# A fused two-layer block on one core: the second expert's columns in their own bank, half of them ahead of the first expert's turn

## Chip, cores and metric

The kernel runs on one core of a Trainium2 chip. The metric is the device time of one execution in microseconds (us), as the median of several. A core has TensorE (PE in the profile, PEld for its weight loads), VectorE (DVE), ScalarE (ACT), GpSimd (POOL) and SyncE (SP), which issues the DMAs. They meet at semaphores.

## What is computed

Two transformer-like layers in fp32 for 256 tokens of width 1024. The first has latent attention, retention, cross attention and a hierarchical mixture of experts, the second a gated recurrence, a short convolution, a SwiGLU block and a per-layer embedding gate. The change is in the mixture of experts:

```python
g_sel = jnp.argmax(g_logits + b_group, axis=-1)              # 1 of 4 groups for a token
e_logits = jnp.take_along_axis(e_all, g_sel[:, None, None], axis=1)[:, 0]
_, top_idx = lax.top_k(e_logits + e_bias, TOP_K)             # 2 of its 8 experts
gate = one_hot(g_sel) * local_w * g_w                        # zero for the other experts
a = jnp.einsum('sd,edf->sef', hr, w_gate)
u = jnp.einsum('sd,edf->sef', hr, w_up)
act = jax.nn.silu(a) * u * gate
return jnp.einsum('sef,efd->sd', act, w_down)                # width 256 inside an expert
```

## The kernel before

**Precision.** Products are done in fp32r. Each operand is split in a high part, rounded to fp32r, and a low part, the rest; a product is three matmuls (`three`, lines 2363 to 2367: high by high, high by low, low by high). The weights come from memory in units of 128 x 2048 floats. ScalarE makes a unit's high part `w_hi` in two halves (`split_hi`, line 440), VectorE its low part `w_lo` in two halves (`split_lo`, line 454), each waiting for the half before it on the other engine. `w_hi` and `w_lo` are rings of three units: the split of unit u waits until TensorE is done with unit u - 3 (`unit_done`). The landing places (`stage`, `first`, `second`, `third`) are six in this stage: SyncE issues the load of a unit once the low part of the unit six before it is ready (`slot_free`, line 395).

**Experts.** Tokens are sorted by group into 128 slots for each of four groups. All eight experts of a group run over the group's 128 slots, so 32 steps in all. An expert has three units: two for the gate and up columns (halves of the 1024 inputs; the 512 result columns of gate and up lie in one PSUM bank, `bank[6]`) and one down unit. Of the first expert (`j` = 0) these are units base, base + 1 and base + 4, of the second base + 2, base + 3 and base + 7: the down unit stands behind the next expert's columns.

A step of TensorE (`step(g, j)`, line 2977) does expert j's columns (24 matmuls), then the down unit of expert j - 1 (12 matmuls into banks 4 and 5), then `turn_hidden`: it transposes expert j's hidden values into bank 7. The columns of the next expert, into bank 6 again, wait for `expert_hidden`, that is until bank 6 is read. ScalarE in the meantime does `tanh` of the gate columns out of bank 6, splits, and copies the turned values to `aT_hi`; VectorE does the two element-wise steps to `silu_g` and `hidden` (lines 2095 and 2097), splits, and makes `aT_lo`.

At g's end `bring_back` multiplies the group's result `y` by the matrix that takes slots to tokens, and adds to banks 0 to 3. These are opened ahead by `open_sums`, a product of a matrix of zeros with `start=True` for each bank: banks 1 to 3 before the first turn, bank 0 after the first down unit, because bank 0 still holds the gates of groups 1 to 3 until ScalarE has copied them (`moe_slot_gates`).

**Order.** `expert_steps` (line 666) writes the order on each engine: steps (0,0) and (0,1) straight; then a loop over g of the steps 2 to 9 (steps 8 and 9 are the next group's first two); then the last group's rest straight. TensorE runs it as a loop of three passes, ScalarE and VectorE have all of it straight. In step (0,0) TensorE also transposes `slot_of` and makes the gates (`turn_gates`), the later ones after ScalarE has kept the gathered tokens of later groups (`later_kept`), which is the last read of banks 0 to 3 from the gathering. In step 0 ScalarE's order is: tanh, split of base + 3, `aT_hi`, gates of groups 1 to 3, two copies to `token_of`; then step 1 with the splits of base + 4 and base + 5, and tanh. VectorE's: `silu_g`, `hidden`, split of base + 3, `aT_lo`; then base + 4, base + 5, `silu_g`, `hidden`.

## Time and profile before

| | us |
|---|---|
| median of three runs | 935.25 |
| lowest and highest | 935.12, 936.57 |
| profiled execution: time | 936.84 |
| profiled execution: its span in the profile | 934.9 |
| TensorE busy | 925.4 |
| VectorE busy | 742.9 |
| ScalarE busy | 625.4 |
| experts' stage on TensorE | about 240 to 521 |

The rows below are from the profiled execution; its time is 1.9 us longer than its span, for what lies around it. A row of a timeline gives start, duration, engine, line, operation, output and inputs, shapes and a count; in brackets stands how long the engine was idle before it, and whom it waited for. Matmuls are pipelined: the duration of one (0.39 us for 512 columns) holds its latency, and the distance between starts, some 0.23, is what the engine takes.

### The profile page before, as it was taken

To read this page: it belongs to the slowest core of one execution; us is meant where nothing else is said; L and a number is where in the kernel's file an instruction comes from. 1 tells how busy PE (TensorE), PEld (TensorE's weight loads), DVE (VectorE), ACT (ScalarE), POOL (GpSimd) and SP (SyncE) were. 2 spreads that over 40 slices of the span, in tenths; PEclk is the share of its full clock that TensorE was granted. 3 is DMA by queue.
4 is the path that set the end of the run, shared out by engine and by line. 5 is a ranking of instruction groups with operands and counts; after the bars stand their busy time and mean duration, and the time that the engine had idled before them with its cause. 6 is when DMAs were issued, how large, how long until landed. Compare 5 with 4: busy or idle time off the path is not lost.

```text
span 934.9 us, 13599 instructions
## 1 busy us (share of the span) xinstructions
PE 925.4 (99%) x5025; PEld 801.7 (86%) x5025; DVE 742.9 (79%) x1111; ACT 625.4 (67%) x953; POOL 20.5 (2%) x41
## 2 busy tenths in 40 slices
PE   9999999999999999999999999999999999999997
PEld 7888888888888888888888899999998888888886
DVE  6667687678999999999999889898897655555576
ACT  6685686676878778788777765747575544434456
POOL 2500000000000000000000000000000000000000
PEclk9999999999999999999999999999999999999999
DMA  9755427523799999999999364737457566555531
GB/s 341 243 183 187 148 91 253 174 70 136 250 371 372 354 363 374 356 366 375 353 365 325 99 198 157 251 114 243 154 186 244 184 201 198 180 180 180 187 129 45
DMA packets 102766, 214.50 MB, mean 229 GB/s; under 512 B 5672, under 2 KB 60480, under 8 KB 97088
## 3 DMA queue, kind: packets, MB, share of 16 engines
q1 hardware_dynamic: 101072, 211.70, 65.3%
q0 software_dynamic: 1344, 2.01, 0.8%
q8 instruction: 26, 0.43, 0.2%
q10 hardware_dynamic: 304, 0.20, 0.1%
q14 instruction: 20, 0.16, 0.0%
HBM read 212.84 MB, written 1.05 MB: 229 GB/s over the span
## 4 chain that ended last, share of the span: by engine, by line
PE 93%; DMA 2%; DVE 2%; ACT 1%; SPq 0%; issue 0%; DVEq 0%; ACTq 0%
PE bank L2367 20%; PE bank L2365 20%; PE bank L2366 20%; PE bank L3196 6%; PE bank L3198 6%; PE bank L3197 6%; PE bank L2382 4%; DMA stage<-in_cross_w_kv_dram 2%; PE bank L2378 2%; PE bank L2372 2%; PE bank L2373 1%; PE bank L2718 1%; PE bank L3223 0%; PE bank L3224 0%; PE bank L3222 0%; DVE w_lo L467 0%
## 5 line engine op out<-in xcount | busy, mean ns | idle before, releaser
L2365 PE MATMUL bank<-w_hi,xT_hi 128*128 128x512 f32 (+2 forms) x626 | 246.9, 394 | 0.0
L2367 PE MATMUL bank<-w_hi,xT_lo 128*128 128x512 f32 (+2 forms) x626 | 242.3, 387 | 0.0
L2366 PE MATMUL bank<-w_lo,xT_hi 128*128 128x512 f32 (+2 forms) x626 | 242.1, 387 | 0.0
L2367 PEld LDWEIGHTS bank<-w_hi,xT_lo 128*128 128x128 f32 x626 | 117.6, 188 | 24.0
L2365 PEld LDWEIGHTS bank<-w_hi,xT_hi 128*128 128x128 f32 x626 | 118.1, 189 | 21.9 <-DVE w_lo L467 0.2
L2366 PEld LDWEIGHTS bank<-w_lo,xT_hi 128*128 128x128 f32 x626 | 117.8, 188 | 22.0
L465 DVE TENSOR_TENSOR w_lo<-stage,w_hi 128x1024 fp32r<-128x1024 f32 (+3 forms) x94 | 107.4, 1142 | 30.2 <-ACT w_hi L451 28.8
L3196 PE MATMUL bank<-hT_hi,w_hi 128*128 128x256 f32 x440 | 123.7, 281 | 0.0
L3198 PE MATMUL bank<-hT_hi,w_lo 128*128 128x256 f32 x440 | 123.6, 281 | 0.0
L3197 PE MATMUL bank<-hT_lo,w_hi 128*128 128x256 f32 x440 | 123.5, 281 | 0.0
L451 ACT ACTIVATE w_hi<-stage 128x1024 fp32r<-128x1024 f32 (+3 forms) x96 | 95.5, 995 | 31.0 <-PE bank L2367 13.3
L467 DVE TENSOR_TENSOR w_lo<-stage,w_hi 128x1024 fp32r<-128x1024 f32 (+3 forms) x94 | 107.1, 1139 | 0.0
L452 ACT ACTIVATE w_hi<-stage 128x1024 fp32r<-128x1024 f32 (+3 forms) x96 | 94.8, 987 | 0.0
L446 ACT ACTIVATE w_hi<-stage 128x1024 fp32r<-128x1024 f32 x55 | 58.2, 1058 | 42.6 <-PE bank L2367 42.3
L459 DVE TENSOR_TENSOR w_lo<-stage,w_hi 128x1024 fp32r<-128x1024 f32 x54 | 65.8, 1219 | 25.1 <-ACT w_hi L446 25.0
L3196 PEld LDWEIGHTS bank<-hT_hi,w_hi 128*128 128x128 f32 x440 | 83.0, 189 | 0.0
L3197 PEld LDWEIGHTS bank<-hT_lo,w_hi 128*128 128x128 f32 x440 | 83.0, 189 | 0.0
L3198 PEld LDWEIGHTS bank<-hT_hi,w_lo 128*128 128x128 f32 x440 | 83.0, 189 | 0.0
L2367 PE MATMUL bank<-w_hi,aT_lo 128*128 128x512 f32 x204 | 79.7, 391 | 0.0
L2365 PE MATMUL bank<-w_hi,aT_hi 128*128 128x512 f32 x204 | 79.6, 390 | 0.0
L2366 PE MATMUL bank<-w_lo,aT_hi 128*128 128x512 f32 x204 | 79.4, 389 | 0.0
L461 DVE TENSOR_TENSOR w_lo<-stage,w_hi 128x1024 fp32r<-128x1024 f32 x54 | 65.8, 1219 | 0.0
(488 smaller groups left out, 1520.8 us busy)
## 6 DMA issues: line engine op xcount, KB each, us to landing
stage<-in_w_in_dram SPq DMA_DIRECT2D x36, 1024.0 KB, 5.2
stage<-in_w_gate_up_dram SPq DMA_DIRECT2D x44, 512.0 KB, 4.7
stage<-in_expert_w_gate_dram SPq DMA_DIRECT2D x33, 512.0 KB, 5.5
stage<-in_expert_w_up_dram SPq DMA_DIRECT2D x33, 512.0 KB, 6.4
second<-in_expert_w_down_dram SPq DMA_DIRECT2D x16, 1024.0 KB, 6.8
stage<-in_expert_w_down_dram SPq DMA_DIRECT2D x15, 1024.0 KB, 7.1
stage<-in_w_down_dram SPq DMA_DIRECT2D x11, 1024.0 KB, 4.8
stage<-in_w_out_dram SPq DMA_DIRECT2D x8, 1024.0 KB, 6.0
```

The source lines that it names most:

```text
L451: nc.scalar.activation(w_hi[:, s, 0:half], src[:, 0:half], ACT.Copy).then_inc(st.half_ready, 1)
L452: nc.scalar.activation(w_hi[:, s, half:cols], src[:, half:cols], ACT.Copy).then_inc(st.hi_ready, 1)
L459: nc.vector.tensor_tensor(beside(w_lo, s, 0), of_both(st, u0, 0), beside(w_hi, s, 0).bitcast(F32), ALU.subtract)
L461: nc.vector.tensor_tensor(beside(w_lo, s, 1), of_both(st, u0, 1), beside(w_hi, s, 1).bitcast(F32), ALU.subtract).then_inc(st.lo_ready, 1)
L465: nc.vector.tensor_tensor(w_lo[:, s, 0:half], src[:, 0:half], w_hi[:, s, 0:half].bitcast(F32), ALU.subtract)
L467: nc.vector.tensor_tensor(w_lo[:, s, half:cols], src[:, half:cols], w_hi[:, s, half:cols].bitcast(F32), ALU.subtract).then_inc(st.lo_ready, 1)
L2365: mm(o, k_hi, v_hi, start=start, stop=False)
L2366: mm(o, k_hi, v_lo, start=False, stop=False)
L2367: return mm(o, k_lo, v_hi, start=False, stop=stop)
L3196: mm(o, w_hi[:, s, at:at + P], hT_hi[:, k, :], start=k == 0, stop=False)
L3197: mm(o, w_hi[:, s, at:at + P], hT_lo[:, k, :], start=False, stop=False)
L3198: ins = mm(o, w_lo[:, s, at:at + P], hT_hi[:, k, :], start=False, stop=k == KD - 1)
```

## The change

The second expert of the first group (`second_expert`: main stream, g the integer 0, j = 1) gets bank 3 for its columns; ScalarE and VectorE read it there. TensorE does the first half of them at the end of step (0,0), before the turn of the first expert's hidden values, and the second half at the head of step (0,1), with no wait for `expert_hidden`. On ScalarE and VectorE the split of the first down unit (base + 4) moves from the head of step (0,1) into step (0,0), behind the split of base + 3 and ahead of `aT_hi` and `aT_lo`. `open_sums` and its four products of zeros are gone: the first `bring_back` starts each bank itself. For that g must be a plain integer in the first pass, so TensorE's first pass over the loop is written out (`peeled=1`), and the loop runs over the two others. The wait for `moe_slot_gates` moves ahead of the first `bring_back`.

```diff
--- before.py
+++ after.py
@@ -663,7 +663,7 @@
 
 
 
-    def expert_steps(eng, groups, step, tail, straight=False):
+    def expert_steps(eng, groups, step, tail, straight=False, peeled=0):
 
         step(0, 0)
         step(0, 1)
@@ -672,7 +672,10 @@
                 for j in range(2, PER_GROUP + 2):
                     step(g, j)
         elif groups > 1:
-            with eng.Fori(0, groups - 1) as g:
+            for g in range(peeled):
+                for j in range(2, PER_GROUP + 2):
+                    step(g, j)
+            with eng.Fori(peeled, groups - 1) as g:
                 for j in range(2, PER_GROUP + 2):
                     step(g, j)
         for j in range(2, PER_GROUP - 1):
@@ -708,6 +711,14 @@
         return k // 2 * 2 + 2
 
     EMBED_ORDER = ((1, 0), (1, 1), (0, 0), (0, 1))
+
+    def second_expert(st, g, j):
+
+        return st is main and isinstance(g, int) and (g, j) == (0, 1)
+
+    def expert_columns(st, g, j):
+
+        return bank[3 if second_expert(st, g, j) else 6]
 
     def gate_bank(g):
 
@@ -1417,12 +1428,14 @@
                 act.wait_ge(st.unit_done, g * PER_TURN + (up_unit(base, j) + 1))
                 if j == PER_GROUP:
                     act.wait_ge(sem(name + "_slot_gates"), 2)
-                nc.scalar.activation(silu_t[:, 0], bank[6][:, 0:FF], ACT.Tanh,
+                nc.scalar.activation(silu_t[:, 0], expert_columns(st, g, j)[:, 0:FF], ACT.Tanh,
                                      scale=slot_gates[:, bass.ds(scale_column(g, j), 1)]).then_inc(sem("expert_tanh"), 1)
                 if j == LAST and next_up:
                     next_high(g, 1)
                 if next_up:
                     split_hi(act, SLOT, up_unit(base, j + 1), PER_TURN, g, st)
+                    if second_expert(st, g, j + 1):
+                        split_hi(act, SLOT, up_unit(base, 1) + 1, PER_TURN, g, st)
                 if last_down_unit is not None and splits[0]:
                     splits[0]()
                 act.wait_ge(sem("expert_turned"), eighths(g, e0 + j + 1))
@@ -1436,7 +1449,7 @@
                     nc.scalar.activation(y_hi[:, c], by_block(bank[4 + c]), ACT.Copy).then_inc(sem("expert_y_hi"), 1)
 
             def step(g, j):
-                if j:
+                if j and not second_expert(st, g, j):
                     split_hi(act, SLOT, up_unit(base, j) + 1, PER_TURN, g, st)
                 if j or st is not main:
                     split_hi(act, SLOT, gate_unit(base, j + 1), PER_TURN, g, st)
@@ -2092,14 +2105,17 @@
                 if last_down_unit is not None:
                     chunk_lo(dve, last_down_unit, 0, st)
                 dve.wait_ge(sem("expert_tanh"), eighths(g, e0 + j + 1))
-                stt(silu_g[:, 0], silu_t[:, 0], 1.0, bank[6][:, 0:FF], ALU.add, ALU.mult).then_inc(sem("expert_silu"), 1)
+                columns = expert_columns(st, g, j)
+                stt(silu_g[:, 0], silu_t[:, 0], 1.0, columns[:, 0:FF], ALU.add, ALU.mult).then_inc(sem("expert_silu"), 1)
                 dve.wait_ge(sem("expert_silu"), eighths(g, e0 + j + 1))
-                stt(hidden[:, 0], bank[6][:, FF:2 * FF], slot_gates[:, bass.ds(gate_column(g, j), 1)], silu_g[:, 0],
+                stt(hidden[:, 0], columns[:, FF:2 * FF], slot_gates[:, bass.ds(gate_column(g, j), 1)], silu_g[:, 0],
                     ALU.mult, ALU.mult).then_inc(sem("expert_hidden"), 1)
                 if j == LAST and next_up:
                     next_low(g, 1)
                 if next_up:
                     split_lo(dve, SLOT, up_unit(base, j + 1), PER_TURN, g, st)
+                    if second_expert(st, g, j + 1):
+                        split_lo(dve, SLOT, up_unit(base, 1) + 1, PER_TURN, g, st)
                 if last_down_unit is not None:
                     chunk_lo(dve, last_down_unit, 1, st).then_inc(st.lo_ready, 1)
                 dve.wait_ge(sem("expert_aT_hi"), eighths(g, e0 + j + 1))
@@ -2120,7 +2136,7 @@
                     tt(dst, dst, bank[n][:, :], ALU.add).then_inc(sem(signal), 1)
 
             def step(g, j):
-                if j:
+                if j and not second_expert(st, g, j):
                     split_lo(dve, SLOT, up_unit(base, j) + 1, PER_TURN, g, st)
                 if j or st is not main:
                     split_lo(dve, SLOT, gate_unit(base, j + 1), PER_TURN, g, st)
@@ -2890,12 +2906,12 @@
                         ins = mm(bank[6][:, :], xg_lo[:, kk], w_hi[:, s, at:at + 512], start=False, stop=kk == KD - 1)
                     ins.then_inc(st.unit_done, 1)
 
-            def columns_of(half, u0, g):
+            def columns_of(half, u0, g, j):
                 pe.wait_ge(st.lo_ready, g * PER_TURN + (u0 + 1))
-                s = u0 % RING
+                s, o = u0 % RING, expert_columns(st, g, j)[:, :]
                 for k in range(4):
                     kk = 4 * half + k
-                    ins = three(bank[6][:, :], xg_hi[:, kk], xg_lo[:, kk], w_hi[:, s, 512 * k:512 * k + 512],
+                    ins = three(o, xg_hi[:, kk], xg_lo[:, kk], w_hi[:, s, 512 * k:512 * k + 512],
                                 w_lo[:, s, 512 * k:512 * k + 512], start=kk == 0, stop=kk == KD - 1)
                 ins.then_inc(st.unit_done, 1)
 
@@ -2949,40 +2965,35 @@
                 for c in range(2):
                     pe.wait_ge(sem("expert_y_hi"), g * 2 + (c + 1))
                     for t in range(T):
-                        mm(bank[2 * c + t][:, :], tokens[t], y_hi[:, c], start=False, stop=False)
+                        mm(bank[2 * c + t][:, :], tokens[t], y_hi[:, c], start=isinstance(g, int) and g == 0, stop=False)
                     pe.wait_ge(sem("expert_y_lo"), g * 2 + (c + 1))
                     for t in range(T):
                         ins = mm(bank[2 * c + t][:, :], tokens[t], y_lo[:, c], start=False, stop=last)
                         if last:
                             ins.then_inc(sem(name + "_returned"), 1)
 
-            def open_sums(banks):
-
-                for n in banks:
-                    mm(bank[n][:, :], zeros[:, 0:P], slot_of[:, 0], start=True, stop=False)
-
             def gate_up(g, j):
-                if j:
+                if j and not second_expert(st, g, j):
                     pe.wait_ge(sem("expert_hidden"), eighths(g, j))
                 if j == PER_GROUP:
                     pe.wait_ge(sem(name + "_moved"), g * 2 + 1)
                 if j == 0:
                     first_columns((gate_unit(base, j), up_unit(base, j)), g)
                     return
-                columns_of(0, gate_unit(base, j), g)
+                if not second_expert(st, g, j):
+                    columns_of(0, gate_unit(base, j), g, j)
                 if j == PER_GROUP:
                     pe.wait_ge(sem(name + "_moved"), g * 2 + 2)
-                columns_of(1, up_unit(base, j), g)
+                columns_of(1, up_unit(base, j), g, j)
 
             def step(g, j):
                 gate_up(g, j)
                 if j == PER_GROUP + 1:
+                    if isinstance(g, int) and g == 0:
+                        pe.wait_ge(sem(name + "_slot_gates"), 2)
                     bring_back(g)
                 if j:
                     down(g, j - 1, up_unit(base, j) + 1)
-                    if j == 1:
-                        pe.wait_ge(sem(name + "_slot_gates"), 2)
-                        open_sums((0,))
                 else:
                     pe.wait_ge(sem("places_known"), 2 * T + 1)
                     for n in range(groups):
@@ -2995,7 +3006,7 @@
                     turn_gates(range(1))
                     pe.wait_ge(sem("later_kept"), KD)
                     turn_gates(range(1, groups))
-                    open_sums((1, 2, 3))
+                    columns_of(0, gate_unit(base, 1), g, 1)
                 turn_hidden(g, j)
 
             def tail(g):
@@ -3005,7 +3016,7 @@
                 down_by_chunks(g, last_down(base, groups))
                 bring_back(g, last=True)
 
-            expert_steps(pe, groups, step, tail)
+            expert_steps(pe, groups, step, tail, peeled=1)
 
         flags = []
         experts("moe", main, U_MOE, GROUPS)
```

## Rows read from the trace of the kernel before

**Rows 1.** Page of the profile, busy time of the engines

```profile
PE 925.4 (99%) x5025; PEld 801.7 (86%) x5025; DVE 742.9 (79%) x1111; ACT 625.4 (67%) x953; POOL 20.5 (2%) x41
```

**Rows 2.** Busy by stretch: us, PE, PEld, DVE, ACT, POOL, PEclk, DMA share, GB/s

```profile
257.70:266.10 8.40, 8.40 (x41) 6.98 (x40) 8.37 (x10) 6.67 (x8) 0.00 (x0) 1.00 1.01 368
```

**Rows 3.** Waits, 230 to 300 us: engine, waited for: us in total, times, longest

```profile
PEld bank L2382 <- DVE hidden L2097: 0.6, 2, 0.4
```

**Rows 4.** Timeline of PE: start us, us, engine, line, op, tiles, count, idle before

```profile
247.83 0.95 PE L2962 MATMUL bank<-slot_of,zeros 128*128 128x512 f32 x3
...
248.78 0.51 PE L2382 MATMUL bank<-const,hidden 128*128 128x128 f32 x2
...
249.04 0.48 PE L2365 MATMUL bank<-w_hi,xT_hi 128*128 128x512 f32 x1
...
254.60 0.39 PE L2365 MATMUL bank<-w_hi,aT_hi 128*128 128x512 f32 x1
...
257.32 0.40 PE L2962 MATMUL bank<-slot_of,zeros 128*128 128x512 f32 x1
...
257.55 0.39 PE L2382 MATMUL bank<-const,hidden 128*128 128x128 f32 x2
...
257.70 0.48 PE L2365 MATMUL bank<-w_hi,xT_hi 128*128 128x512 f32 x1
```

**Rows 5.** Timeline of ACT (ScalarE), 247 to 251 us

```profile
247.33 1.05 ACT L446 ACTIVATE w_hi<-first 128x1024 fp32r<-128x1024 f32 x1
...
248.28 1.05 ACT L448 ACTIVATE w_hi<-first 128x1024 fp32r<-128x1024 f32 x1
...
249.33 0.39 ACT L1430 ACTIVATE aT_hi<-bank 128x256 fp32r<-128x256 f32 x1
...
249.70 1.10 ACT L1450 ACTIVATE token_of<-bank 128x512 fp32r<-128x512 f32 x2
...
250.65 1.08 ACT L451 ACTIVATE w_hi<-second 128x1024 fp32r<-128x1024 f32 x1
```

**Rows 6.** Timeline of DVE (VectorE), 246 to 257 us

```profile
246.66 1.22 DVE L461 TENSOR_TENSOR w_lo<-stage,w_hi 128x1024 fp32r<-128x1024 f32 x1
...
249.78 1.22 DVE L461 TENSOR_TENSOR w_lo<-first,w_hi 128x1024 fp32r<-128x1024 f32 x1
...
250.91 0.42 DVE L2107 TENSOR_TENSOR aT_lo<-bank,aT_hi 128x256 fp32r<-128x256 f32 x1
...
251.77 1.23 DVE L465 TENSOR_TENSOR w_lo<-second,w_hi 128x1024 fp32r<-128x1024 f32 x1 [0.44 <-ACT w_hi L451]
...
256.32 0.41 DVE L2095 SCALAR_TENSOR_TENSOR silu_g<-silu_t,bank 128x256 f32<-128x256 f32 x1
...
256.77 0.48 DVE L2097 SCALAR_TENSOR_TENSOR hidden<-bank,slot_gates,silu_g 128x256 f32<-128x256 f32 x1
```

**Rows 7.** Timeline of DVE and PEld at the fourth expert's turn

```profile
273.79 0.48 DVE L2097 SCALAR_TENSOR_TENSOR hidden<-bank,slot_gates,silu_g 128x256 f32<-128x256 f32 x1
...
274.33 0.31 PEld L2382 LDWEIGHTS bank<-const,hidden 128*128 128x128 f32 x2 [0.20 <-DVE hidden L2097]
```

**Rows 8.** Timeline of DVE, its next wait after 251.77

```profile
295.62 1.22 DVE L459 TENSOR_TENSOR w_lo<-stage,w_hi 128x1024 fp32r<-128x1024 f32 x1 [0.18 <-ACT w_hi L446]
```

**Rows 9.** Loads into `second`, 245 to 520 us, from issue to landing

```profile
DMA to landing us min/median/max: 4.8/6.7/8.3
```

**Rows 10.** Timeline of PE around a loop edge and the loop's exit

```profile
316.77 0.48 PE L2365 MATMUL bank<-w_hi,xT_hi 128*128 128x512 f32 x1
...
327.07 0.48 PE L2365 MATMUL bank<-w_hi,xT_hi 128*128 128x512 f32 x1
...
455.48 0.48 PE L2365 MATMUL bank<-w_hi,xT_hi 128*128 128x512 f32 x1
...
465.79 0.48 PE L2365 MATMUL bank<-w_hi,xT_hi 128*128 128x512 f32 x1
```

**Rows 11.** DMA queues, 240 to 325 us: packets, MB, share of 16 engines

```profile
q8 instruction: 4, 0.07, 0.3%
```

## Prediction

> **What bounds the kernel now.** I read the page first: TensorE is busy for 925.4 of 934.9 us [rows 1], so only what lies on its own path can move the end. Then the busy times by stretch: inside the experts' stage TensorE is never idle, its clock is the full 2.4 GHz (granted 1.00), VectorE is busy for 8.37 of 8.40 us and the DMA engines are full (share 1.01) [rows 2]. So there are three candidates for a bound, and the question is which of them the change meets next. Then the waits of TensorE, of which the second expert's start holds one of 0.4 us, on the first expert's hidden values [rows 3]. Last the three engines' timelines between 246 and 258 us, where nearly all of the change happens.
>
> I call the experts' units U+0, U+1 (first expert's columns), U+2, U+3 (second's), U+4 (first down unit), U+5, U+6 (third's columns), U+7 (second down unit).
>
> TensorE now ends the gate products, opens three banks with products of zeros at 247.83, waits for `hidden` and turns it at 248.78, starts the second expert's columns at 249.04, the first down unit at 254.60, opens bank 0 at 257.32, turns the second hidden at 257.55 and starts the third expert at 257.70 [rows 4]. A dozen products without a restart takes 257.32 - 254.60 = 2.72 us; the dozen after a turn takes 254.60 - 249.04 - 2.72 = 2.84. Where the turn is late, its first weight load starts 0.06 us after `hidden` ends (274.33 against 273.79 + 0.48) [rows 7] and the columns 0.26 after the turn (249.04 - 248.78), 0.32 in all. A turn that isn't late takes 257.70 - 257.55 = 0.15.
>
> **The products of zeros and the idle time.** Between 247.83 and 248.78 lie three products of zeros and a wait, 0.95 us, and bank 0's product costs 257.55 - 257.32 = 0.23 [rows 4]. The most that can go is 1.18 us. The `start` flag that replaces them is on products that are issued anyway, and the wait for the slot gates, moved to `bring_back`, is met some 60 us before: ScalarE has those copies behind it when it starts `token_of` at 249.70 [rows 5]. Both at nothing.
>
> **Half the second expert's columns ahead of the turn.** They need U+2's low parts: the last VectorE half of it starts at 246.66 and takes 1.22, so 247.88 [rows 6]; with 0.06 for the signal TensorE starts at 247.94 instead of 247.83. Then 2.84 to 250.78. Bank 3 instead of 6 is what makes this free of the readers of bank 6; bank 3's own last readers are the copies to `later`, for which the gate products wait already. The turn follows at 250.78 without a wait. The other half needs U+3's low parts: 249.78 + 1.22 = 251.00 [rows 6], so it starts at 251.06, not at 250.93: 0.13 lost. It ends at 253.90.
>
> **The down unit's split ahead of the turned values.** On ScalarE the halves of U+3 start at 247.33 and 248.28, 0.95 apart [rows 5]. U+4 follows at 249.23 and 250.18, not at 250.65 [rows 5]; its ring place was free since the first columns ended. Queued behind it is now the copy `aT_hi`: the turn at 250.78 plus 0.43 gives 251.21, and ScalarE is free at 251.13, so nothing waits. That copy and the gates take 0.37 (249.33 to 249.70), the two `token_of` copies 0.95: ScalarE starts U+5 at 252.53 and, at some 1.07 a half, the first is there at 253.60. VectorE does U+4 from 250.91 (its place after U+3 [rows 6]), two halves of 1.14 to 253.19; behind them is `aT_lo`, 0.34, to 253.53, so the first down unit has its operand at 253.61 (the write takes 0.42). TensorE arrives there at 253.90: the margin is 0.29. VectorE then waits to 253.64 for U+5's high half: 0.11 idle where it now has 0.44 by its row and 0.52 by its starts [rows 6]. U+5 ends at 253.64 + 2.28 = 255.92, where `silu_g` starts; now it starts at 256.32. **VectorE is 0.40 us ahead, and no more**: its work is the same, only this gap closed. The tanh stands behind U+5's halves on ScalarE, at about 254.4 (the columns are done by then), and U+5's low halves hide it.
>
> **TensorE after it.** The down unit ends at 253.90 + 2.72 = 256.62; `hidden` of the second expert is ready 0.40 earlier, 256.77 + 0.48 - 0.40 = 256.85, so the third expert starts at 256.85 + 0.32 = 257.17 instead of 257.70: 0.53 gained, with the wait for zeros gone and one for VectorE in its place. Without that wait it would be 256.77, 0.93 gained.
>
> **What is late next.** From 251.77 to beyond 274 VectorE works without a gap (the next wait that its timeline shows is at 295.62 [rows 8]), and at 274.33, ahead of the fifth expert, `hidden` is already what comes last [rows 7]. There TensorE can gain only what VectorE gained: 0.40. By 295.62 VectorE has begun to wait for the others, and all moves together. The sum: -1.18 (zeros and wait) - 0.11 (the turn is not late: 0.15, not 0.26) + 0.11 (U+2) + 0.13 (U+3) + 0.12 (a restart, 2.84 for 2.72) + 0.40 (`hidden`, second expert) + 0.13 (`hidden`, fourth) = -0.40 us. For the profiled execution, 936.84 - 0.40 = 936.44; that execution lies 1.6 us above the median of the runs, 935.25, from which I count: 934.85.
>
> **Weights.** U+4's place in the stage comes free at 253.27 instead of 254.13, so its next load is issued 0.86 earlier, the others up to 0.4. A load into `second` lands within 8.3 us at most [rows 9], and a place is filled again every six units, two steps of some 8.4 us. Even with the engines full this doesn't bind, and the view of the waits has no split in this stage behind a landing. Nothing.
>
> **The peeled code.** Eight steps of TensorE stand straight ahead of the loop. Step to step, the pass over the loop's edge takes 327.07 - 316.77 = 10.30 us, and leaving the loop for straight code 465.79 - 455.48 = 10.31 [rows 10]: the edge costs nothing, and one edge less gives nothing. The copy must be fetched: four instruction blocks over 85 us took 0.3% of 16 engines, about 1.0 us each [rows 11], and the timeline shows no gap of TensorE at them. The copy adds three or four such blocks, in the same full DMA load. I take nothing; the bounds are below nothing by 0.1 (register work of the waits) and above by 4 us.
> The Trainium skill, "Runtime: NRT & Kernel Launch", section "Instruction fetch mechanics", says that a taken branch out of the window of fetched pages stalls for a fetch, and that kernels prefer unrolling for this. By it one edge less would be worth a fetch; the two passes of [rows 10] do not agree with it for this loop. The same section says that sequential prefetch mostly hides a block's crossing, which speaks against the rival of slow fetches; the straight parts here agree.
>
> **Rivals.**
> - A, all waits vanish: TensorE gains 0.95 to 1.18, 934.1 to 934.3. It needs VectorE to be shorter too; its unbroken row of work speaks against it.
> - B, nothing is gained: the copies on ScalarE (`aT_hi`, `token_of`) come later than I place them, U+5's split with them, and VectorE's gap is only moved. If U+5's first half is 0.40 us later, the whole gain is gone: 935.25. The margins of 0.1 to 0.3 us above speak for it, that each step has its row speaks against it.
> - C, slower: the blocks of the peeled copy arrive late under full DMA queues. It decides once a block lands later than TensorE's lead; three or four blocks of 1.0 us less 0.40 give +2.6 to +3.6: 938 to 939. The straight first pass of now, with its four blocks and no gap, speaks against it.
> - D, a back edge costs a fetch after all and one less gives about 1.0 more: 935.25 - 0.40 - 1.0 = 933.85. The rule of the "Instruction fetch mechanics" section above would have it so.
>
> **How the numbers follow.** Forecast 0.70, A 0.07, B 0.14, C 0.04, D 0.03, the rest 0.02. The three runs of before span 1.45 us, more than the gain, so the range takes in A and B with some 0.3 to 0.8 us of scatter: 934.0 to 936.0. A measurement of this kernel can tell about 0.2%, 1.9 us, from no change; the forecast, A, B and D lie within it (D at its edge with scatter). So faster 0.02, same 0.93, slower 0.05.
>
> **What the profile after would show.** Second expert's first product at about 247.9 into its own bank; no products of zeros; the turn at 250.8; a wait of 0.3 us or so before the turn at 256.9 for `hidden`; third expert at 257.2; fifth expert at 274.2; from there every row 0.4 us earlier, with about 8.4 us a step. VectorE without the 0.44 gap. Four instruction blocks more and no gap of TensorE beside them. It is wrong if a gap stands beside a block, if the third expert starts later than 257.7, or if the lead at 330 us isn't the lead at 520.

## The result: 0.22% slower, and a profile that hides why

| | before | changed |
|---|---|---|
| median of nine runs, us | 935.27 | 938.06 |
| lowest and highest | 934.81, 936.57 | 936.37, 939.35 |
| profiled execution, time and span | 936.84, 934.9 | 936.37, 934.5 |

The ratio is 1.0022, 95% interval 1.0013 to 1.0030: 2.8 us slower, where 0.4 us faster was forecast, and outside the range. Yet the profiled execution of the changed kernel is the quickest of its nine runs, 0.47 us below that of before. So the profile has to be read piece by piece.

**The piece that the change is about came out as summed.** TensorE's timeline of the changed kernel, 246 to 257 us (start, duration, engine, line, operation, count, idle before):

```profile
246.78 0.82 PE L2888 MATMUL bank<-token_gates,slot_of 128*128 128x16 f32 x6
247.52 0.50 PE L2381 MATMUL bank<-w_hi,xT_hi 128*128 128x512 f32 x1
...
250.39 0.39 PE L2398 MATMUL bank<-const,hidden 128*128 128x128 f32 x2
250.63 0.50 PE L2381 MATMUL bank<-w_hi,xT_hi 128*128 128x512 f32 x1
...
253.50 0.39 PE L2381 MATMUL bank<-w_hi,aT_hi 128*128 128x512 f32 x1
...
256.53 0.50 PE L2398 MATMUL bank<-const,hidden 128*128 128x128 f32 x2
256.79 0.48 PE L2381 MATMUL bank<-w_hi,xT_hi 128*128 128x512 f32 x1
```

They answer to [rows 4]. This execution was already 0.38 us ahead when it came to the experts (its first gate product starts at 245.743, that of before at 246.127), which isn't the change's. With 0.38 added, the second expert's columns start at 247.90 (said: 247.94), their second half at 251.01 (251.06), the down unit at 253.88 (253.90), the third expert at 257.17 (257.17). The products of zeros are gone. VectorE's and ScalarE's rows of the same stretch, which answer to [rows 5, 6]:

```profile
252.77 0.42 DVE L2123 TENSOR_TENSOR aT_lo<-bank,aT_hi 128x256 fp32r<-128x256 f32 x1
253.26 1.23 DVE L459 TENSOR_TENSOR w_lo<-third,w_hi 128x1024 fp32r<-128x1024 f32 x1
...
255.54 0.41 DVE L2109 SCALAR_TENSOR_TENSOR silu_g<-silu_t,bank 128x256 f32<-128x256 f32 x1
255.99 0.48 DVE L2111 SCALAR_TENSOR_TENSOR hidden<-bank,slot_gates,silu_g 128x256 f32<-128x256 f32 x1
```

```profile
250.81 0.39 ACT L1443 ACTIVATE aT_hi<-bank 128x256 fp32r<-128x256 f32 x1
...
252.14 1.09 ACT L446 ACTIVATE w_hi<-third 128x1024 fp32r<-128x1024 f32 x1
```

VectorE's idle time ahead of the split, marked 0.44 in [rows 6], is no longer marked; `hidden` is the last to come for the turn, as forecast. And the row that answers to [rows 7]: VectorE hands over `hidden` at 273.01 + 0.48, and TensorE has waited 0.33 for it.

```profile
273.54 0.32 PEld L2398 LDWEIGHTS bank<-const,hidden 128*128 128x128 f32 x2 [0.33 <-DVE hidden L2111]
```

To compare executions without their different starts I take the time from the first gate product to the last product of a `token_now` behind the experts: 521.19 - 246.13 = 275.06 us before, 520.46 - 245.74 = 274.72 changed. **The stage is 0.34 us shorter**; the sum said 0.40.

**The loss lies behind the stage.** TensorE, 520 to 526 us, first before, then changed:

```profile
520.85 0.73 PE L2955 MATMUL bank<-xT_lo,token_now 128*128 128x512 f32 x2
522.04 2.29 PE L2382 MATMUL bank<-const,x 128*128 128x128 f32 x16 [0.46 <-DVE x L2120]
524.09 0.36 PE L3208 MATMUL bank<-hT_hi,w_hi 128*128 128x256 f32 x1
```

```profile
520.12 0.74 PE L2971 MATMUL bank<-xT_lo,token_now 128*128 128x512 f32 x2
521.32 1.74 PE L2398 MATMUL bank<-const,x 128*128 128x128 f32 x11 [0.46 <-DVE x L2136]
525.04 0.71 PE L2398 MATMUL bank<-const,x 128*128 128x128 f32 x5 [1.98 <-issue]
525.50 0.36 PE L3219 MATMUL bank<-hT_hi,w_hi 128*128 128x256 f32 x1
```

Sixteen transposes follow one another; only the ninth's weight load waits, 0.34 us for VectorE's `x`. Before, they run through; now TensorE stops after the eleventh, for 1.98 us, and the reason given is "issue": nothing that the profile knows was waited for. From start to start the gap is 525.04 - 522.78 = 2.26 us, where 0.11 is usual. Nothing in the diff touches these lines. The lead of 0.72 us (522.04 against 521.32) turns into a lag of 1.41 (524.09 against 525.50).

**Why the profiled time hides it.** Busy times by stretch of the heads' stage, first before, then changed:

```profile
531.00:696.00 165.00, 165.00 (x1390) 164.88 (x1389) 144.38 (x211) 106.61 (x146) 0.00 (x0) 1.00 0.59 190
```

```profile
531.00:696.00 165.00, 164.91 (x1402) 164.58 (x1401) 145.06 (x216) 107.75 (x147) 0.00 (x0) 1.00 0.59 191
```

With TensorE busy throughout in both and the same clock, the execution of before did 1390 products in 165 us, that of the changed kernel 1402: 118.6 ns a product against 117.3, by the mean distance of their starts with the few pauses left out. From its first product to its last the stage takes 171.34 us in the one (524.09 to 695.43) and 169.50 in the other (525.50 to 695.00), 1.8 us less, and that has nothing to do with the change: of the fourteen executions profiled in this study three have the short spacing (the changed kernel here, e2 and e7, 117.3 to 117.5) and eleven the long one (118.4 to 118.7), and the changed kernel, profiled again as e8, had the long one. So the two profiles' difference of -0.47 is -0.72 (lead) + 2.13 (stop, from lead to lag) - 1.8 (spacing), and -0.1 that I leave unassigned. What the change is worth is told by the medians of nine runs, not by the two profiled executions.

### The profile page after: what moved, and what is told of

It reads as the page before. It is cut to its first block, busy times and chain, and to the rows that moved or that the text cites. A ratio compares the mean times of both kernels' runs of the same rounds, so it can differ in the third digit from the quotient of the medians.

```text
span 934.5 us, 13561 instructions
## 1 busy us (share of the span) xinstructions
PE 922.5 (99%) x5021; PEld 798.9 (85%) x5021; DVE 742.8 (79%) x1111; ACT 625.5 (67%) x953; POOL 20.6 (2%) x41
## 4 chain that ended last, share of the span: by engine, by line
PE 93%; DVE 3%; ACT 2%; issue 1%; DMA 0%; DVEq 0%; ACTq 0%
PE bank L2383 20%; PE bank L2381 20%; PE bank L2382 20%; PE bank L3207 5%; PE bank L3208 5%; PE bank L3209 5%; PE bank L2398 4%; PE bank L2394 3%; PE bank L2388 2%; PE bank L2389 2%; PE bank L2734 1%; DVE w_lo L467 1%; DMA silu_g<-in_mem_norm_g_dram 0%; DVE w_lo L465 0%; PE bank L2461 0%
```

## What stops TensorE there

Behind the experts stands code for tokens that don't fit their group's slots: two branches (lines 3102 and 3105 of the changed kernel, 3091 and 3094 before) jump over it when there are none, as here. Between the last `token_now` product and the transposes TensorE therefore takes two jumps. In the built file of TensorE's program an instruction is 64 bytes, and the trace's queue 8 ("instruction") brings packets of 16,384 bytes, so blocks of 256 instructions. I counted from the head of that file where the jump lands: at instruction 4177 before, with 175 instructions left in that block; at 4810 in the changed kernel, 633 further on because of the peeled steps, with 54 left. TensorE stopped after eleven transposes. Each is two instructions (weights, product), so 22 of the 54 are theirs; a label and a wait ahead of the first, a wait ahead of the ninth, and the weight load of the twelfth (which is done ahead of the stop) make 26.

So TensorE stops 28 instructions ahead of the place where the count puts the block's end. The same 28 remain in e1 (17 of 45 done), e3 (27 of 55) and e6 (42 of 70) below. I read this as the end of a block all the same, at the same place in every kernel, and as a count that begins 28 instructions late: in the running program every place lies 28 further on in its block than in the file. What the 28 are isn't on record. "Left", in the names of the runs and in the expectations, is the count of the file.

The theories ahead of the first experiments were:
- Theory 1: the block behind the one that the jump lands in is asked for too late, and comes some 3.7 us after TensorE goes on there. Position alone decides.
- Theory 2: the moved work does it, by other transfers at that time.
- Theory 3: peeling as such does it, by the number of blocks to be brought.

## Experiments on the cause

**e1: the peeled steps alone.** The kernel before with one pass of TensorE's loop written straight, all else as it was:

```diff
-            with eng.Fori(0, groups - 1) as g:
+            for g in range(peeled):
+                for j in range(2, PER_GROUP + 2):
+                    step(g, j)
+            with eng.Fori(peeled, groups - 1) as g:
...
-            expert_steps(pe, groups, step, tail)
+            expert_steps(pe, groups, step, tail, peeled=1)
```

> The kernel before with TensorE's first pass over the experts' loop written out, nothing else; it does 642 instructions more for TensorE, and the jump over the unused overflow code lands 45 instructions ahead of the end of its block of 256. Theory 1 (the next block is asked for only when the one landed in is entered, and comes some 3.7 us later): TensorE stops for 2.0 to 2.7 us amid the transposes behind the experts, as in the changed kernel, and the time is 1.9 us above before, or 3.6 where the clock falls after the gap: 937.2 to 939. Theory 2 (the gap belongs to the moved columns, their waits or the first products that now start the banks): no gap, 935.3. Theory 3 (the peeled steps themselves run slower, as rival C of the prediction had it): steps of more than 8.43 us between 257 and 327, no gap behind the experts.

Measured: 940.61 us against 936.91 of the kernel before, measured beside it, ratio 1.0047 (1.0032 to 1.0062), more than theory 1 had said. TensorE stops for 3.14 us from start to start (said: 2.0 to 2.7), earlier among the transposes, with 45 instructions left:

```profile
521.53 0.98 PE L2385 MATMUL bank<-const,x 128*128 128x128 f32 x7 [0.46 <-DVE x L2123]
525.38 1.18 PE L2385 MATMUL bank<-const,x 128*128 128x128 f32 x9 [2.86 <-issue]
```

The seven transposes are 14 of the 45; with the label, the wait and the eighth weight load 17 are done, and 28 are over: the stop is at the same place of a block again. Its stage takes 275.06 us, exactly that of before: the peeled steps give nothing in themselves, and one back edge less is worth nothing.

**e2: the moved work alone.** The changed kernel with TensorE's loop whole, so that the banks are opened by products of zeros as before:

```diff
-            expert_steps(pe, groups, step, tail, peeled=1)
+            expert_steps(pe, groups, step, tail)
...
+                    open_sums((1, 2))
```

> The change without the peel: the second expert's columns in bank 3, half of them ahead of the first turn, the down unit's split ahead of the turned values, but the loop of three passes kept and the four products of zeros too (banks 1 and 2 ahead of those columns, bank 0 ahead of the second turn, bank 3 behind it). The place of the code behind the experts is as before, to one instruction. Theory 1: no gap behind the experts; the third expert starts about 0.25 us earlier and the end moves by -0.2 to -0.3: 935.0. Theory 2: a gap of about 2 us behind the experts, 937 or more. Theory 3: as theory 1.

Measured: 935.78 against 936.91, ratio 0.9997 (0.9989 to 1.0006), no gap behind the experts. The stage takes 275.10 us: the gain of the stage is gone too, where 0.2 to 0.3 us had been expected to stay. Its rows say why: two products of zeros now stand ahead of the columns, the turn comes later, and ScalarE and VectorE wait for it.

```profile
247.61 0.71 PE L2978 MATMUL bank<-slot_of,zeros 128*128 128x512 f32 x2
```

```profile
253.80 1.23 DVE L459 TENSOR_TENSOR w_lo<-third,w_hi 128x1024 fp32r<-128x1024 f32 x1 [0.42 <-ACT w_hi L446]
```

This is the forecast's rival B at work in another kernel: VectorE's gap of 0.44 [rows 6] is only moved, to 0.42, and with it all of the gain. The 0.34 us needs both, the moved work and the products of zeros gone.

**e3: the kernel before, shifted.** Nothing of the change; satisfied waits (240 of them, which make 120 instructions; below I name the instructions) among the last group's steps put the jump's target to where 55 instructions are left:

```diff
+        def spare_waits():
+            for _ in range(min(spare[0], spare[1])):
+                pe.wait_ge(lo_ready, 1)
+                spare[1] -= 1
...
             mm(o, k_hi, v_hi, start=start, stop=False)
+            spare_waits()
             mm(o, k_hi, v_lo, start=False, stop=False)
+            spare_waits()
```

> The kernel before with nothing changed but 120 extra instructions of TensorE's sequencer, waits that are long satisfied, between the products of the last group's steps; they move the jump over the overflow code to the same place in its block as in the changed kernel (it lands 55 instructions ahead of a block's end, there 54, before 175). Theory 1: a gap of about 2.2 us amid the transposes behind the experts, time 1.9 to 3.6 us above before: 937.2 to 938.9. Theories 2 and 3: no gap, 935.3 (up to 0.3 more if the waits cost anything).

Measured: 939.05 against 936.91, ratio 1.0025 (1.0015 to 1.0036), and a stop of 2.73 us (one of the last four transposes is missing in the trace's records):

```profile
522.00 1.85 PE L2392 MATMUL bank<-const,x 128*128 128x128 f32 x12 [0.46 <-DVE x L2120]
526.31 0.90 PE L2392 MATMUL bank<-const,x 128*128 128x128 f32 x3 [2.45 <-issue]
```

**The loss of the change is had here without the change.** The stage takes 275.06 us, so the waits themselves cost nothing.

**e4: the changed kernel, shifted.** The same waits in the changed kernel leave 190 instructions.

> The changed kernel with the same 120 satisfied waits in the last group's steps: the jump now lands 190 instructions ahead of a block's end. Theory 1: no gap behind the experts, and what the prediction summed is left: 0.4 us below before, 934.9. Theories 2 and 3: the gap or the loss is there as in the changed kernel, 938.

Measured: 936.14 against 936.91, ratio 0.9992 (0.9983 to 1.0000); all 16 transposes in one row of 2.29 us, no stop; the stage takes 274.75. Theories 2 and 3 fall: the moved work and the peeled steps are both in this kernel.

**e5, e6, e7: other positions.** The same edit with 40 waits in the changed kernel (14 instructions left), with 105 in the one before (70 left), and with 70 in the changed one (240 left).

> The changed kernel with 40 more satisfied waits in the straight steps of the last group on TensorE: the place that TensorE jumps to behind the overflow code then has 14 instructions left in its block of 256, where the changed kernel has 54. Theory 1 (the block behind the jump's target is asked for only as the target's block is entered, and comes 3.7 to 4.3 us after TensorE goes on there, whatever is left): the stop begins earlier, 0.3 to 0.5 us after the first transpose behind the jump in place of 1.5, and is longer, 3.2 to 3.9 us in place of 2.26; a fall to half clock behind it; 938.5 to 941. Rival (a stop of one size, whatever is left): 2.3 us again, and 938.

> The kernel before with 105 satisfied waits in the straight steps of the last group on TensorE, so that 70 instructions are left in the block of the jump's target, where e3 had 55. Theory 1: the block's end is passed some 0.5 to 0.7 us later than in e3 (four more transposes and some three of the products of the first head), and the next block comes at the same time, so the stop is 1.4 to 2.2 us and lies among the first products of the heads, not among the transposes. Rival (one size): 2.7 us again. Time: with a fall to half clock behind the stop 937.5 to 939, without one 936.5 to 937.5.

> The change whole, with 70 satisfied waits, so that 240 instructions are left in the block of the jump's target (e4: 120 waits and 190 left). Theory 1: no stop behind the jump, no fall of the clock there, and the change's own 0.35 to 0.40 us in the experts' stage is kept: 0.3 to 0.5 us under the kernel before of the same chip, as e4 gave 0.8 by the medians. Rival (e4's waits themselves took the stop away, by giving the fetch more time before the jump): with 70 in place of 120 some of the stop comes back, over 0.5 us.

Measured, e6: 938.20 against 936.47, ratio 1.0018 (1.0009 to 1.0028). The stop is 1.55 us and stands where it was expected, behind sixteen transposes and three products (38 of the 70 instructions; with the label and three waits 42 are done, and again 28 are over):

```profile
522.21 2.29 PE L2392 MATMUL bank<-const,x 128*128 128x128 f32 x16 [0.46 <-DVE x L2120]
...
524.58 0.28 PE L3220 MATMUL bank<-hT_hi,w_hi 128*128 128x256 f32 x1
526.12 0.39 PE L3221 MATMUL bank<-hT_hi,w_lo 128*128 128x256 f32 x1 [1.27 <-issue]
```

e5: 939.89, ratio 1.0039 (1.0026 to 1.0052). The stop is at the jump itself and 4.17 us long (5.02 from the last product, of which 0.85 is usual); I had said 3.2 to 3.9 and behind some transposes. The 28 explain it: the 14 left by the file's count are none, the target lies 14 instructions into the next block, and TensorE wants that block at once.

e7 missed altogether: 941.40, ratio 1.0048 (1.0033 to 1.0062), the worst of all, where no stop was expected. TensorE stops at the first transpose, 4.19 us beyond the usual 0.85:

```profile
520.48 0.73 PE L2981 MATMUL bank<-xT_lo,token_now 128*128 128x512 f32 x2
525.86 3.65 PE L2408 MATMUL bank<-const,x 128*128 128x128 f32 x16 [4.65 <-issue]
```

So the instructions left behind the target don't decide alone. By the file's count the first branch is here 4 instructions ahead of the end of block 17 (counted from 0), the second lies in block 18, the target in block 19. Theory 1 becomes theory P: **a block is asked for when TensorE enters the one ahead of it, one block at a time**. A jump out of block 17 to the second branch enters block 18, block 19 is asked for then, and where the target lies in it TensorE wants it at once.

With the 28 added this is e5's case, not e7's. In e5 the first branch lies 6 instructions ahead of the end of block 17, the second in block 18, the target 14 instructions into block 19. In the changed kernel and in e1 the second branch is likewise the first place in block 18, and block 19 is wanted 26 and 17 instructions behind the target; in e3 and e6 the same holds two blocks lower, with 27 and 42. In e4 the branches' block is entered 73 instructions ahead of the first branch, in a straight line, and block 19's packet starts at 510.78, before any jump. All this fits theory P. **e7 fits it only in part**: its block 18 is entered 23 instructions ahead of the first branch (by the count its first product there starts at 517.99, 2.8 us before the last one ahead of the jump), the data queues are all but idle from 516 to 520 us (share 0.03), and yet block 19's packet starts behind the jump, at 523.22. The expectations of e10 to e12 leave the 28 out.

**e8: the changed kernel again**, for the rest of its loss: a stop of 2.26 us less the stage's 0.34 is less than 2.8.

> The changed kernel once more, for the part of its loss that is not the stop. Theory 1: the same stop at the same place, 2.0 to 2.6 us among the 16 transposes behind the experts; and where the time is near its median (937.5 to 938.5) a stretch of 3.4 us at half clock right behind the stop, which costs about 1.7 us, and which the first profile of it (936.37) did not have. Rival (the loss of the median is elsewhere): a profile of a run near 938 without a half clock there.

Measured: 939.43 against 936.47, ratio 1.0034 (1.0024 to 1.0044). The same stop after the same eleven transposes, now 2.56 us, and the granted clock at half behind it, for 6.83 us where 3.4 had been expected. The profiled run is the slowest of the ten (940.81). Timeline, then stretches of it (busy us of PE, PEld, DVE, ACT, POOL, then PEclk):

```profile
521.34 1.74 PE L2398 MATMUL bank<-const,x 128*128 128x128 f32 x11 [0.46 <-DVE x L2136]
525.37 1.22 PE L2398 MATMUL bank<-const,x 128*128 128x128 f32 x5 [2.29 <-issue]
...
528.95 0.41 PE L3219 MATMUL bank<-hT_hi,w_hi 128*128 128x256 f32 x1
529.16 0.41 PE L3220 MATMUL bank<-hT_hi,w_lo 128*128 128x256 f32 x1
```

```profile
520.00:522.81 2.81, 2.25 (x13) 1.43 (x13) 2.48 (x5) 2.03 (x5) 0.00 (x0) 1.00 1.03 354
522.81:525.37 2.56, 0.28 (x4) 0.14 (x2) 1.66 (x4) 0.79 (x3) 0.00 (x0) 0.77 0.04 9
525.37:526.60 1.23, 1.23 (x6) 1.23 (x6) 0.00 (x0) 0.82 (x2) 0.00 (x0) 0.50 0.06 13
526.60:530.00 3.40, 3.40 (x17) 3.40 (x17) 3.35 (x6) 3.37 (x12) 0.00 (x0) 0.50 0.00 0
```

The clock falls from 2.4 to 1.2 GHz at 524.19, inside the stop, and is back at 531.02. The last five transposes take 1.22 us in place of 0.71, and the products follow at 0.21 us in place of 0.12. From 525.37 to 531.02 that costs some 5.65 x (1 - 0.119/0.213) = 2.5 us. Against the profiled execution of before, which has the same spacing in the heads, the parts are -0.70 (lead at the transposes) + 2.45 (stop) + 2.5 (clock) = 4.2; the spans differ by 938.9 - 934.9 = 4.0. The first profile of the changed kernel (mean clock 0.999) had no such fall; its other eight runs are 1.4 to 3.0 us longer, with mean clocks of 0.996 or 0.997 in six of them and 0.998 in two (a half clock in the span's last 4 to 6 us, as in the profile of before, makes 0.998 alone). Part of the eight's distance can also be the long spacing of the heads, 1.8 us, which the first profile did not have either.

**e9: is the block itself held up?** In every profile with a stop, the missing block's packet starts close to the end of a load of 1 MB. This kernel cuts that load to an eighth; the first head then works on stale weights for one of its units, and so its output is another.

```diff
+                elif h == 0 and j == 3:
+                    load_unit(sp, w_in2[:, 0:1, bass.ds(h * 256 + group * D, 256)], 256, u)
```

> The changed kernel, with the 1 MB load of the fourth input unit of the heads (issued at 518.40, its packets from 519.44 to 522.95 in the profile of the changed kernel) cut to an eighth of its rows; the rest of that unit is stale, so the first head is computed from wrong weights. In the six profiles with a stop the packet of the missing block (queue 8, 16 KB) starts within 0.5 us of the end of this load, and TensorE goes on 2.4 to 2.7 us after it starts. Theory L (the block waits behind the load): the packet starts right after the jump, at 521.4 to 521.7, and the stop shrinks by 0.9 to 1.1 us to 1.2 to 1.6 us, with no half clock behind it; 936.0 to 937. Theory F (a fixed time from the jump to the packet, 1.2 to 1.8 us, that only happens to end with the load): the stop stays 2.0 to 2.6 us, and 938 to 939.5.

Measured: 936.98 against 936.71, ratio 1.0006 (0.9997 to 1.0015), and the stop shrinks from 2.26 and 2.56 to 1.14 us (said: 1.2 to 1.6), with no half clock behind it:

```profile
521.42 1.74 PE L2400 MATMUL bank<-const,x 128*128 128x128 f32 x11 [0.46 <-DVE x L2138]
524.04 0.71 PE L2400 MATMUL bank<-const,x 128*128 128x128 f32 x5 [0.87 <-issue]
```

The queues from 521.2 us on show it, first of the changed kernel (to 522.4), then of e9 (to 521.5; packets, MB, share of 16 engines):

```profile
q1 hardware_dynamic: 454, 0.46, 109.2%
```

```profile
q8 instruction: 1, 0.02, 26.7%
```

With the load cut, the block's packet starts at 521.32; with it, the data packets fill the engines first, and the block's starts at 522.53. **Theory L holds: the block waits behind the load, and that is about 1.2 us of the stop.** All ten runs of e9 lie between 936.83 and 937.65, so none has the 2 us of a fallen clock.

**e10, e11, e12: where theory P says that it is safe.** e10 has 78 waits, 8 more than e7, so that by the file's count the first branch lies fourth in block 18, and with the 28 added 31 instructions behind its start; e11 has 154 (also in the tail's steps), e12 is e4 again.

> The change whole, with 78 waits where e7 had 70: every jump and target lies 8 instructions further on. e7's first branch was 4 instructions ahead of its block's end, its second branch in the next block and its target in the block behind that, 4.19 us late. Here the first branch is the fourth instruction of the block in which the second one lies too. Theory P (a block is asked for when TensorE's reader enters the one ahead of it in a straight line, and a branch near a block's end keeps the reader out of the next): here the reader enters ahead of the branch, so the target's block is asked for before the jump: no stop or one under 1.5 us, 934.5 to 937. Rival J (nothing ahead of a branch counts, a block is asked for only by the jump into the one before): a stop of 3 to 4.2 us at the first transpose as in e7, 939.5 to 941.5.

> The change whole with 154 waits: the two branches lie 69 and 137 instructions into one block, the target is the 101st instruction of the next, and 156 are left in it. Theory P: the target's block was asked for 69 instructions ahead of the branch, and at the 0.06 us that an instruction takes in the heads' products the 156 left last over 5 us, against 3.7 to 4.3 us until the block behind comes: no stop, as in e4, and the change keeps its 0.35 to 0.40 us: 0.3 to 0.6 us under the kernel before of the same chip. Rival (e4 was an accident of its one chip): a stop of some size, and no gain.

> e4 once more (120 waits, 190 instructions left), beside the kernel before of another call: a ratio of 0.9992 again, that is 0.3 to 0.8 us under it, if the stop is all that the change lost; 1.000 or more if e4's ratio was chance.

Measured, e10: no stop in the profiled execution, and its block came early. The timeline's row, then queue 8 from 516.8 to 517.0 us:

```profile
521.54 2.29 PE L2408 MATMUL bank<-const,x 128*128 128x128 f32 x16 [0.46 <-DVE x L2136]
```

```profile
q8 instruction: 1, 0.02, 39.3%
```

The packet of block 19 starts at 516.89, ahead of the branches (e7: 523.22, behind them). But of its ten runs six are 934.39 to 936.53 and four 940.21 to 941.85, e7's times, and one of e7's twelve is 934.47. So eight instructions turn the usual case round, and close to the edge it goes either way from run to run; only the median (936.50, ratio 1.0018, 1.0002 to 1.0035) hides that.

Theory P's order holds in every profile: a block's packet starts only when TensorE is about to enter the one ahead of it, or has entered it. Its moment doesn't hold: after an entry 23 instructions ahead of the first branch the block was late in eleven of twelve runs (e7), after 31 in four of ten (e10), and after 73 and 97 (e4 and e12, e11) none of 35 runs has a time like e7's. Rival J is right for e7 and for those four runs of e10. Whether the block is asked for only some dozens of instructions behind the entry, or a jump drops a request that is under way, wasn't tested.

e11: 936.50 against 936.71, ratio 0.9998 (0.9990 to 1.0007), no stop, stage 274.72; under the kernel before by less than said, and not by more than chance. e12: 934.88 against 936.71, ratio 0.9988 (0.9980 to 0.9997); stage 274.70. e4's interval ended at 1.0000; by both measurements this kernel is at or a little under the one before, and it is faster than the changed one by more. How much of its gain is more than the stage's 0.34 us (0.04%, inside both intervals) the runs don't tell.

**All positions in one table.** "On" is where TensorE goes on behind the jump, or would have, 0.85 us after its last product; the packet is that of the missing block (in the last row the last one ahead of the jump), its start read from the trace's packets; "again" is where TensorE goes on behind the stop.

| kernel | left by the file | less 28 | on | packet | again | stop | packet to again |
|---|---|---|---|---|---|---|---|
| changed | 54 | 26 | 521.32 | 522.53 | 525.04 | 2.26 | 2.51 |
| e8, the same | 54 | 26 | 521.34 | 522.88 | 525.37 | 2.56 | 2.49 |
| e1 | 45 | 17 | 521.53 | 523.01 | 525.38 | 3.14 | 2.37 |
| e3 | 55 | 27 | 522.00 | 523.76 | 526.31 | 2.73 | 2.55 |
| e6 | 70 | 42 | 522.21 | 523.68 | 526.12 | 1.55 | 2.44 |
| e5 | 14 | block of target | 521.25 | 522.76 | 525.42 | 4.17 | 2.66 |
| e7 | 240 | block of target | 521.67 | 523.22 | 525.86 | 4.19 | 2.64 |
| e9, load cut | 54 | 26 | 521.42 | 521.32 | 524.04 | 1.14 | 2.72 |
| before, e2, e4, e11, e12, e10 profiled | 156 to 232 | 128 to 204 | | 510.6 to 516.9 | | none | |

The packet takes 1.1 to 1.3 us, and the block is of use 2.4 to 2.7 us after its start, whatever else differs.

## Why the prediction was wrong

**The failed step is "The peeled code".** It named its price rightly: the trace of before showed nothing of a late block, and the bounds went up to 4 us. It then took "nothing", because the loop's edge and the straight passage show no gap [rows 10, 11], and left the upper bound out of the range. Both readings were right, and e1 repeats them: no gap at the edges, none at the peeled blocks, a stage of 275.06 us. The trace brings three blocks more (29 packets on queue 8 for 26), within the three or four of the prediction, and one of its own signs of being wrong came true: a gap that a late block makes. But I had looked for the price where the code was added. It fell due 200 us later, at a jump that the diff doesn't touch, because 633 instructions more had moved it against the blocks. Rival C had the mechanism (a block that comes late under a full load) and was given 0.04 for the wrong place; that its size fits (2.6 to 3.6 us; measured 2.8) is luck, since it summed three or four late blocks of 1.0 us, and the runs have one late block and half clock behind it; what spoke against it there, the straight first pass without a gap, said nothing of a jump.

The rule of the Trainium skill, "Runtime: NRT & Kernel Launch", section "Instruction fetch mechanics", that a taken branch out of the window of two pages stalls for a fetch (its pages are the blocks here), I had weighed at the loop's back edge only, where the trace doesn't show it. At the jumps behind the experts the traces agree with it (e5: 4.17 us, e7: 4.19), and with its statement that the next page is fetched while the current one runs (e4: packet at 510.78 us, 11 us ahead of the transposes). These runs add a case: a jump to a block which is there costs 1.55 to 3.14 us when it lands 42 to 17 instructions ahead of that block's end.

**The right steps.** The sum of the stage, -0.40, measured -0.34: each of its starts within 0.05 us. That VectorE gains only its own gap, and TensorE with it: e2 shows the reverse, with the gap moved and the gain at nothing. The products of zeros at 1.18 with their wait: removing them is what keeps the turn from being late. The wait of 0.3 us for `hidden` at the fifth expert: 0.33. Weights: nothing, as said. The loop's edge: nothing. Rival D fell with e1.

**The missing term** is then +2.1 to +2.4 us of stop and, in most runs, 1.5 to 2.5 us of half clock behind it. In the profiled execution of the changed kernel only the first is there. The 2.5 are measured in e8, the 1.5 are an estimate, e8's spacings over the 3.41 us that the clock stayed down in e1 and e3. That the clock makes up the rest of the median's 2.8 us (1.0 us, beside a stop of 2.13 and the stage's -0.34) is not shown: of the nine runs only mean clocks are known, and neither the length of a fall nor the spacing of the heads.

## What to carry to other kernels

Code added ahead of a branch isn't paid where it stands: count, before and after, where each branch and each target behind it lies in the blocks of 256 instructions. A count from the file's head can be off by a constant, 28 instructions here; the place of one stop gives it. Then see that the branches' block is entered well ahead of them (73 and 97 instructions were enough, 31 only mostly, 23 hardly ever) and that the target's block goes on long enough behind it (128 instructions were enough, 42 were not). A gap put down to "issue" amid instructions that wait for nothing, in a place that the diff doesn't touch, is a reason to count; a hundred or so satisfied waits in covered places moved it, at no cost here. And a change of 0.4 us is not to be judged from one profiled execution of each kernel when a stage of both can differ by 1.8 us between executions.

## What the runs showed of the hardware

- An instruction block asked for at a jump was of use 3.7 to 4.3 us after TensorE went on there (seven profiles), with a load of 1 MB under way, and 2.6 us after it with that load cut (e9). From its packet's start to the first instruction it was 2.4 to 2.7 us in all of them; the transfer is 1.1 to 1.3 us of it.
- A loop of some 670 instructions ran without bringing its blocks again: in the kernel before queue 8 has no packet from 320.18 to 485.90 us, in which the second and the third pass lie.
- A stop of TensorE of 2.56 us or more was followed by half clock for 3.41 us (e1, e3) or 6.83 us (e5, e7, e8) in each of the five profiles that had one; after stops of 1.14, 1.55 and 2.26 us (e9, e6, the changed kernel) the clock stayed at 2.4 GHz.
- Products of 256 columns in the heads' stage follow each other at some 117.3 or at some 118.6 ns, one value for a whole execution, at a granted clock of 1.00 both times. The runs of the kernel before lie in two groups, around 935.1 and 936.8 us, which fits it. What sets it wasn't tried.
